# A two-layer hybrid block on one core: the retention's group norm from centred values and mean squares, its output parts added on TensorE

## What is computed

```python
def _retention(q, k, v, g, gn_w, gn_b, cos, sin):      # 4 heads of 64, 8 chunks of 128 tokens
    inner = jnp.einsum('bnihd,bnjhd->bnhij', qc, kc) * decay
    inner = jnp.einsum('bnhij,bnjhe->bnihe', inner, vc)
    # state carried over the chunks: k'v, with a decay
    cross = jnp.einsum('bnihd,nbhde->bnihe', qc, prev_states) * xi[None, None, :, :, None]
    o = (inner + cross).reshape(b, s, h, dv)
    mu = jnp.mean(o32, axis=-1, keepdims=True)
    var = jnp.mean(jnp.square(o32 - mu), axis=-1, keepdims=True)
    o = ((o32 - mu) * lax.rsqrt(var + RET_GN_EPS)).astype(dt).reshape(b, s, RET_WIDTH)
    o = o * gn_w + gn_b
    return jax.nn.silu(g) * o
```

## Time and profile before

| what | value |
|---|---|
| time, median of 3 runs | 2645.51 us (2643.24 to 2648.67) |
| the profiled execution's own time | 2646.41 us |
| its span | 2644.6 us |
| PE busy | 2555.4 us, 97% of the span |
| PEld busy | 2191.1 us, 83% |
| DVE busy | 1531.2 us, 58% |
| ACT busy | 1095.3 us, 41% |
| POOL busy | 1013.6 us, 38% |

### The profile page before, as it was taken

One profiled execution on the slowest core, in us unless ns is written; L12 is line 12 of the kernel. 1 busy time (PEld: TensorE's weight loads), 2 busy tenths in 40 slices (PEclk: granted clock), 3 DMA queues, 4 the chain that ended last, 5 costly groups with the idle time before them and its releaser, 6 DMA issues. The chain is left out here.

```text
span 2644.6 us, 43326 instructions
## 1 busy us (share of the span) xinstructions
PE 2555.4 (97%) x13188; PEld 2191.1 (83%) x13188; DVE 1531.2 (58%) x3045; ACT 1095.3 (41%) x2503; POOL 1013.6 (38%) x1161
## 2 busy tenths in 40 slices
PE   7999989999999999999999999999999999999997
PEld 6999977878788888888889998777887888888886
DVE  4667555472654455577647775555627454545785
ACT  4444554372522332344444455444634232223444
POOL 2455422174254545201044555222723545451012
PEclk8999999999999999999999999999999999999999
DMA  5111011014233233573321101012222233327533
GB/s 182 29 34 35 20 38 39 28 66 152 68 108 114 80 115 107 181 264 96 104 100 33 46 19 42 5 39 86 87 86 91 85 112 110 100 91 261 195 97 122
DMA packets 238651, 242.68 MB, mean 92 GB/s; under 512 B 27904, under 2 KB 171008, under 8 KB 238464
## 3 DMA queue, kind: packets, MB, share of 16 engines
q1 hardware_dynamic: 238464, 240.43, 28.1%
HBM read 172.75 MB, written 67.63 MB: 91 GB/s over the span
## 5 line engine op out<-in xcount | busy, mean ns | idle before, releaser
L2470 POOL TENSOR_TENSOR fw_a_lo<-fw_a_raw,fw_a_hi 128x512 fp32r<-128x512 f32 x132 | 178.8, 1355 | 457.6 <-DVE fw_s_raw L2053 457.6
L2470 POOL TENSOR_TENSOR fw_s_lo<-fw_s_raw,fw_s_hi 128x512 fp32r<-128x512 f32 x176 | 230.9, 1324 | 53.6 <-ACT fw_s_hi L1543 53.6
L733 PE MATMUL banks<-ht_hi,da_hi 128*128 128x512 f32 x496 | 193.2, 390 | 0.0
L733 PE MATMUL banks<-ht_lo,da_hi 128*128 128x512 f32 x496 | 193.2, 390 | 0.0
L733 PE MATMUL banks<-ht_hi,da_lo 128*128 128x512 f32 x496 | 193.2, 390 | 0.0
L733 PE MATMUL banks<-w_diff_hi,ht_hi 128*128 128x384 f32 x512 | 181.2, 354 | 6.1 <-DVE ht_lo L1730 4.1
L733 PE MATMUL banks<-w_diff_hi,ht_lo 128*128 128x384 f32 x512 | 173.5, 339 | 0.0
L733 PE MATMUL banks<-w_diff_lo,ht_hi 128*128 128x384 f32 x512 | 173.2, 338 | 0.0
L2298 POOL TENSOR_TENSOR qk_rot<-rope_a,rope_b 128x512 f32<-128x512 f32 x64 | 82.7, 1292 | 204.1 <-DVE rope_b L1759 204.1
L1787 DVE TENSOR_REDUCE stats<-banks 128x1 f32<-128x1024 f32 (+3 forms) x192 | 138.5, 749 | 29.3 <-PE banks L944 23.4
L1617 ACT ACTIVATE u_two<-u_two 128x512 f32<-128x512 f32 x42 | 26.6, 632 | 281.7 <-DVE u_two L2164 281.7
(11 more groups left out here) (357 smaller groups left out, 7506.8 us busy)
## 6 DMA issues: line engine op xcount, KB each, us to landing
da_raw<-act_scratch SPq DMA_DIRECT2D x154, 256.0 KB, 2.7
fw_a_raw<-in_w_gate_dram SPq DMA_DIRECT2D x88, 256.0 KB, 3.1
act_scratch<-act_s SPq DMA_DIRECT2D x66, 256.0 KB, 3.0
w_diff_raw<-in_w_in_dram SPq DMA_DIRECT2D x24, 512.0 KB, 6.4
fw_a<-in_w_up_dram SPq DMA_DIRECT2D x44, 256.0 KB, 3.2
fw_a_raw<-in_w_up_dram SPq DMA_DIRECT2D x44, 256.0 KB, 2.9
act_scratch<-act_zero SPq DMA_DIRECT2D x44, 256.0 KB, 2.4
act_scratch<-act_one SPq DMA_DIRECT2D x44, 256.0 KB, 2.8
```

What stands on the lines that cost most here:

```text
L733: mm = pe.matmul(bank, lhsT, rhs, start=first and i == 0, stop=last and i == len(pairs) - 1, skip_group_check=resumes)
L2470: pool.tensor_tensor(w[1][:], w[2][:], w[0][:].bitcast(F32), ALU.subtract).then_inc(S["f_lo"], 1)
```

## The change

The v columns are scaled while ACT copies them, with a sum of each head's 64 columns beside it, and DVE subtracts the mean of them. The output is three matmuls of 64 columns into the same 64 columns of the bank, in place of one of 128 columns and one of 64. ACT copies the sum out (`ret_take`) and squares it once for two units (`ret_squares`); DVE sums the squares, adds epsilon and scales the output (`ret_sums`, `ret_mean_squares`, `ret_normed`); `bn_stats`, `bn_aggr` and the offset are gone. POOL's root no longer adds epsilon, and `ret_finish` runs in rounds 7, 9, ..., 21. The third `keep_clock` of a round is gone; the three matmuls of `first_product` stay.

```diff
@@ TensorE @@
+        def ret_rows(j):
+            return banks[:, RET_OUT[j], 0:RET_DIM]
...
-                    fill(u, 2, RET_OUT[0])
-                    def both_parts(j, hi, lo, sides, first, last):
-                        pe.matmul(banks[:, RET_OUT[j], 0:P].rearrange("p (c d) -> p c d", c=2), hi, sides, start=first, stop=False)
-                        return pe.matmul(banks[:, RET_OUT[j], 0:64], lo, sides[:, 0, :], start=False, stop=last)
+                    if first_products_at(u):
+                        first_product(u, 2)
                     for j in range(2):
-                        mm = both_parts(j, r_at_hi[n % 2][:, tokens(j)], r_at_lo[n % 2][:, tokens(j)], rv[n % 5][:, j], True, t == 0)
+                        mm = products(ret_rows(j), split((r_at_hi[n % 2][:, tokens(j)], r_at_lo[n % 2][:, tokens(j)]),
+                                                            (rv[n % 5][:, j, 0, :], rv[n % 5][:, j, 1, :])), last=t == 0)
...
-                            mm = both_parts(j, rt_hi[n % 3][at_, 0, :], rt_lo[n % 3][at_, 0, :], state[at_, :, at_], False, True)
+                            mm = products(ret_rows(j), split((rt_hi[n % 3][at_, 0, :], rt_lo[n % 3][at_, 0, :]),
+                                                                (state[at_, 0, at_], state[at_, 1, at_])), first=False)
@@ ScalarE @@
-                def ret_normed(n):
...
-                    for j in range(2):
-                        st = act.activation(r_norm[b][:, i, 64 * j:64 * j + 64], r_sum[m % 3][:, i, j, :], ACT.Identity,
-                                            bias=r_nb[:, b, 2 * i + j:2 * i + j + 1], scale=r_rs[:, b, 2 * i + j:2 * i + j + 1])
+                def ret_take(n):
...
+                    act.activation(r_sum[m % 3][:, n % 2], banks[:, RET_OUT[0]:RET_OUT[1] + 1, 0:RET_DIM], ACT.Copy).then_inc(S["r_take"], 1)
+                def ret_squares(m):
...
+                    act.activation(r_square[:], r_sum[m % 3][:], ACT.Square).then_inc(S["r_sq"], 1)
...
-                        act.activation(r_z[n][:], banks[:, Z_BANK, :], ACT.Copy).then_inc(S["z_free"], 1)
+                        act.activation(r_z[n][:, 0:2 * P], banks[:, Z_BANK, 0:2 * P], ACT.Copy)
+                        for j in range(2):
+                            v = slice(2 * P + RET_DIM * j, 2 * P + RET_DIM * (j + 1))
+                            act.activation(r_z[n][:, v], banks[:, Z_BANK, v], ACT.Copy, scale=xz[:, n // T, j:j + 1], accum_out=v_sum[:, n, j:j + 1])
+                        act.activation(r_z[n][:, 3 * P:4 * P], banks[:, Z_BANK, 3 * P:4 * P], ACT.Copy).then_inc(S["z_free"], 1)
@@ VectorE @@
-                    dve.tensor_tensor(v, v, xz[:, n // T, 0:2].unsqueeze(2).to_broadcast([P, 2, RET_DIM]), ALU.mult)
+                    dve.scalar_tensor_tensor(v, v_sum[:, n, :].unsqueeze(2).to_broadcast([P, 2, RET_DIM]), -1.0 / RET_DIM, v, ALU.mult, ALU.add)
...
+                    dve.tensor_reduce(r_ss[:, m % 2], r_square[:], AX_X, ALU.add).then_inc(S["r_ss"], 1)
...
+                    dve.scalar_tensor_tensor(r_ms[:, b], r_ss[:, b], 1.0 / RET_DIM, xz[:, p, 2:4].unsqueeze(1).to_broadcast([P, 2, 2]),
+                                             ALU.mult, ALU.add).then_inc(S["r_ms"], 1)
...
+                    dve.tensor_tensor(r_norm[b][:].rearrange("p i (j d) -> p i j d", j=2), r_sum[m % 3][:],
+                                      r_rs[:, b].unsqueeze(3).to_broadcast([P, 2, 2, RET_DIM]), ALU.mult).then_inc(S["r_on"], 1)
@@ GpSimd @@
-                    pool.tensor_tensor(r_ms[:, b, :].rearrange("p (i j) -> p i j", i=2), mv[:, b, :, 1].rearrange("p (i j) -> p i j", i=2),
-                                       xz[:, p, 2:4].unsqueeze(1).to_broadcast([P, 2, 2]), ALU.add).then_inc(S["r_ms"], 1)
...
-                    if u >= 9 and u % 2 == 1 and u != RET_UNITS - 1:
-                        ret_finish((u - 9) // 2)
-                    if u == RET_UNITS:
-                        ret_finish((u - 10) // 2)
+                    if u >= 7 and u % 2 == 1 and (u - 7) // 2 < RET_UNITS // 2:
+                        ret_finish((u - 7) // 2)
```

More of the change, by code:

```diff
@@ L128 @@
     m_qrope=T, m_cn=T,
-    r_vlo=2 * T, r_take=2 * T, r_nb=T, r_gate=2 * T, r_kzhi=2 * T, r_kzlo=2 * T, ri_done=2 * T, r_at=2 * T, r_athi=2 * T, r_atlo=2 * T,
+    r_vlo=2 * T, r_take=2 * T, r_sq=T, r_ss=T, r_gate=2 * T, r_kzhi=2 * T, r_kzlo=2 * T, ri_done=2 * T, r_at=2 * T, r_athi=2 * T, r_atlo=2 * T,
     ro_done=2 * T, rs_done=2 * (T - 1), r_st=2 * (T - 1), r_sthi=2 * (T - 1), r_stlo=2 * (T - 1),
-    r_bn=2 * T, r_mv=2 * T, r_ms=T, r_rstd=T, r_on=2 * T, r_gw=T, r_gb=T, r_mx=T,
+    r_ms=T, r_rstd=T, r_on=T, r_gw=T, r_gb=T, r_mx=T,
     out_done=2 * T, out_add=2 * T,
@@ L304, in hybrid_block_kernel @@
     r_sum = [sb(f"r_sum{i}", [P, 2, 2, RET_DIM], F32, EREG + (12 + i) * KB) for i in range(3)]
+    r_square = sb("r_square", [P, 2, 2, RET_DIM], F32, EREG + 15 * KB)
     r_st2 = [sb(f"r_st2{i}", [P, 2, P], F32R, HT + (29 + i) * KB) for i in range(3)]
@@ L415, in hybrid_block_kernel @@
     m_rs = small(2, T)
-    bn = small(2, 2, 6)
-    mv = small(2, 4, 2)
-    r_rs = small(2, 4)
-    r_ms = small(2, 4)
-    r_nb = small(2, 4)
+    v_sum = small(2 * T, 2)
+    r_ss = small(2, 2, 2)
+    r_rs = small(2, 2, 2)
+    r_ms = small(2, 2, 2)
     minus_half = small(4)
@@ L1517, in _ @@
                 for u in RET_STEPS:
+                    if 0 <= u - 3 < RET_UNITS:
+                        ret_take(u - 3)
                     if u < RET_UNITS:
@@ L1522, in _ @@
                         ret_gate_and_v(u + 2)
-                    if 0 <= u - 7 < RET_UNITS:
-                        ret_normed(u - 7)
                     if 0 <= u - 1 < RET_UNITS:
                         ret_inner(u - 1)
+                    if u % 2 == 0 and 0 <= u // 2 - 2 < RET_UNITS // 2:
+                        ret_squares(u // 2 - 2)
                     if u in ROUND_OUT:
@@ L1965, in ret_inner, with ret_sums @@
                         st.then_inc(S["r_st"], 1)
-                def ret_take(n):
-                    m, i = n // 2, n % 2
-                    dve.wait_ge(S["ro_done"], L * PER["ro_done"] + n + 1)
-                    if m >= 3:
-                        dve.wait_ge(S["r_on"], L * PER["r_on"] + 2 * (m - 2))
-                    dve.tensor_reduce(r_sum[m % 3][:, i], banks[:, RET_OUT[0]:RET_OUT[1] + 1, 0:P].rearrange("p j (c d) -> p j d c", c=2),
-                                      AX_X, ALU.add).then_inc(S["r_take"], 1)
-                def ret_moments(n):
-                    m, i = n // 2, n % 2
-                    dve.wait_ge(S["r_take"], L * PER["r_take"] + n + 1)
-                    for j in range(2):
-                        st = dve.bn_stats(bn[:, i, j, :], r_sum[m % 3][:, i, j, :])
-                    st.then_inc(S["r_bn"], 1)
-                    dve.wait_ge(S["r_bn"], L * PER["r_bn"] + n + 1)
-                    dve.sem_inc(S["passed"], 1)
-                    for j in range(2):
-                        st = dve.bn_aggr(mv[:, m % 2, 2 * i + j, :], bn[:, i, j, :])
-                    st.then_inc(S["r_mv"], 1)
+                def ret_sums(m):
+                    dve.wait_ge(S["r_sq"], L * PER["r_sq"] + m + 1)
+                    if m >= 2:
+                        dve.wait_ge(S["r_ms"], L * PER["r_ms"] + m - 1)
+                    dve.tensor_reduce(r_ss[:, m % 2], r_square[:], AX_X, ALU.add).then_inc(S["r_ss"], 1)
                 def ret_state_low(n):
@@ L2020, in _ @@
                 for u in RET_STEPS:
-                    if 0 <= u - 3 < RET_UNITS:
-                        ret_take(u - 3)
+                    m = u // 2 - 2
+                    if u % 2 == 1 and 0 <= m < RET_UNITS // 2:
+                        ret_sums(m)
                     if u < RET_UNITS:
                         ret_low(u)
+                    if u % 2 == 1 and 0 <= m < RET_UNITS // 2:
+                        ret_mean_squares(m)
                     if 0 <= u - 1 < RET_UNITS:
                         ret_inner(u - 1)
-                    if 0 <= u - 3 < RET_UNITS:
-                        ret_moments(u - 3)
-                    if u >= 6 and u % 2 == 0 and u // 2 - 3 < RET_UNITS // 2:
-                        ret_offset(u // 2 - 3)
+                    if u % 2 == 0 and 0 <= m - 1 < RET_UNITS // 2:
+                        ret_normed(m - 1)
                     if u + 2 < RET_UNITS:
```

35 lines of the change are left out of this document (19 added, 16 removed).

## The result

| | before | after |
|---|---|---|
| median of 4 runs | 2647.06 us (2643.24 to 2648.67) | 2700.52 us (2695.94 to 2701.63) |
| ratio, 95% interval | | 1.0201 [1.0185, 1.0216] |
| profiled execution, own time | 2646.41 us | 2699.57 us |
| its mean granted clock | 0.992 | 0.974 |

The forecast was 2649.0 us with a range of 2641 to 2655. The kernel became 53.5 us slower.

A forecast was written before the change was run, and what follows sets the result against it. PE, busy for 97% of the span, was taken as the bound. Per layer, rounds -2.3 + 5.1 - 3.5 + 1.2 = +0.5 us and copy +1.2; doubled, +3.4 on 2645.5 gives 2649 us, range 2641 to 2655.

The forecast's parts named there:

- The clock falls: Rival: retention rounds at half clock for 3.4 us stretches, two a layer, +6.8 us on the sum, 2656 us; chance 0.07.
- the wait in round 11: Retention rounds: a new PE wait of 0.5 us for POOL, part of the 1.2 us a layer of new waits.
- The new wait of POOL: Round 9's state product: PE waits 0.7 us for unit 8's rk_lo, queued behind the first ret_finish moved to round 7.
- The third unread matmul: Rounds 2 to 10 and 17: removing it saves 0.23 us each, 2.3 us a layer.
- The output on PE: Retention outputs: extra matmuls paced by weight loads 0.11 us apart, 0.33 us for 14 outputs, 0.22 for two; 5.1 us a layer.
- the waits that go: Rounds 3 to 16: PE's existing waits, about half for DVE and half for POOL, disappear, saving 3.5 us a layer.
- the rival in which the extra matmuls are nearly free: Retention outputs: extra matmuls cost 25 to 30 ns each, 1.6 us a layer, giving 2643 us; chance 0.13.
- The copy in four pieces: MLA steps: ACT's copy takes 1.2 us in place of 0.60, so PE's projections wait, +1.2 us a layer.
- the waits of 0.12 us: MLA steps: three of the five projection waits a layer caused by the longer copy, 0.12 us each.
- The rival with a copy of 1.46 us: MLA steps: bank held 1.46 us, seven intervals become waits, 2.3 us a layer, 2651 us; chance 0.20.
- B: Experiments' theory, retention rounds: the clock's fall follows a single stop of PE, which comes from the order on POOL.
- A: Experiments' theory, retention rounds: the clock falls because PE has less long work with the third unread matmul gone.

The follow-up runs named there:

- kernel 7: kernel 5 with only the first ret_finish moved back to round 7: 2702.70 us, ratio 1.0210.
- kernel 8: The changed kernel with eight unread matmuls put ahead of PE's wait in round 9: 2655.00 us, ratio 1.0032.
- kernel 5: The changed kernel with the third unread matmul back and ret_finish in even rounds from 8: 2653.04 us, ratio 1.0029.
- kernel 6: The changed kernel with ret_finish in even rounds from 8, third unread matmul still out: 2652.17 us, ratio 1.0043.
- kernel 3: The kernel before with only the third unread matmul taken out of rounds 2 to 10 and 17: 2695.11 us, ratio 1.0181.
- kernel 11: The kernel before with the projected unit copied in four pieces with sums and the mean subtracted on DVE: 2646.97 us, ratio 1.0005.
- kernel 1: The changed kernel with the third unread matmul put back in rounds 2 to 10 and 17: 2697.62 us, ratio 1.0192.
- kernel 2: The changed kernel with ret_finish back in its old rounds (9, 11, 13, 16, 17, ...): 2679.16 us, ratio 1.0121.
- kernel 4: The changed kernel with the third unread matmul back and ret_finish in its old rounds: 2677.59 us, ratio 1.0106.
- kernel 12: kernel 5 with the output as before, eight matmuls and the reduction on DVE: 2649.66 us, ratio 1.0015.
- kernel 9: The kernel before with the third unread matmul kept in rounds 2 to 4, out of 5 to 10 and 17: 2647.79 us, ratio 1.0009.

## Why the prediction was wrong

**The step that failed** is the rival "The clock falls". Its mechanism was named and then dismissed at 0.07 with the reason that PE still works for over nine tenths of each round, and it was priced with two stretches of 3.4 us a layer. The share was the wrong thing to look at. In kernel 7 PE is busy for 16.00 us of the 16 from 541 us on (the first row of its table by stretch) and its clock falls behind one wait; kernel 8 has PE's useful work just as late and, by its times, mostly stays up. The size was wrong by more: the clock did not come back after one such stretch, but only 47.8 and 51.2 us later. At half clock a round took 1.80 times as long and not twice (6.34 us against 3.53 in kernel 5), so 0.80 / 1.80 = 0.44 of those 99.0 us is lost, 44 us. To this come 2 x (1.97 - 0.7) = 2.5 us of wait, and 2 x 0.5 = 1.0 us goes, the wait in round 11 that didn't appear: 45.5 us over the forecast of 2649, where 51.5 was measured. The other 6 are not accounted for; kernel 6, without a fall, lies 4 us above my terms as well (below). The reckoning is an estimate; the measurement is that kernel 6, which differs in POOL's order alone, stands 48 us lower, and that the rounds of its profiled execution are 22.9 and 23.6 us shorter in the two layers.

**The new wait of POOL, 0.7 us forecast, 1.97 measured,** was the term that set this off. Two parts of it slipped. I let POOL's start move up to 549.9; the root came at 550.58. And I took the 0.42 us that POOL waited in that stretch out of the sum, since PE would be earlier; it became 1.18 us, because the scores' high part did not come earlier, while POOL did. With these two, 550.58 + 11.2 + 1.18 = 562.96, and `rk_lo` began at 563.06. PE, too, came later to the state product than forecast, at 563.71 - 1.97 = 561.74 in place of 560.8, or the wait would have been 0.9 us longer still. The mistake is to move one engine forward and leave the chain that feeds it (PE, DVE, ACT) where it need not be asked.

**The third unread matmul, 2.3 us a layer:** the rounds of kernels 5 and 6 differ by 61.01 - (599.08 - 538.92) = 0.85 us. Kernel 6 has a wait of 0.81 us that 5 lacks, so the matmuls themselves are worth 1.7. That stretch begins at round 3 and holds nine of the ten, so it is 0.18 us each, and in round 6 alone 3.53 - 3.31 = 0.22, where 0.23 was forecast: the size was about right. What the term left out is that the removal lets PE arrive earlier at places where it then waits: in kernel 3 it turns 0.51 us into 0.74 and that costs 51 us.

**The output on PE and the waits that go.** Kernel 5 keeps the third matmul and has no waits, so my terms give it 5.1 - 3.5 = +1.6 us a layer; its rounds are 61.01 - 59.56 = 1.45 us longer. Its round 6 takes 3.53 us against 3.21, the 0.33 forecast for an output. That also settles the rival in which the extra matmuls are nearly free. In the changed kernel's round 6, on the timeline of PE, they stand as forecast:

```profile
553.18 0.28 PE L737 MATMUL banks<-rv,r_at_lo 128*128 128x64 f32 x1
553.29 0.39 PE L737 MATMUL banks<-rv,r_at_hi 128*128 128x64 f32 x2
553.51 0.28 PE L737 MATMUL banks<-rv,r_at_lo 128*128 128x64 f32 x1
```

From 553.18 to 553.51 three matmuls start, each with a weight load of its own: 0.11 us each, at 64 columns a matmul. The Trainium skill, page "TensorE: Matmul & The Clock Gate", section "Back-to-back issue gap", gives the 25 ns for a matmul by itself and says that in a stream of weight loads and matmuls both set the spacing. Here it is the spacing of the section "LDWEIGHTS" that the trace agrees with.

**The copy in four pieces, 1.2 us a layer.** The timeline of ACT in the changed kernel:

```profile
480.14 0.38 ACT L1497 ACTIVATE r_z<-banks 128x256 f32<-128x256 f32 x1 [1.95 <-PE banks L737]
480.42 0.31 ACT L1500 ACTIVATE r_z<-banks,stats 128x64 f32<-128x64 f32 x1
480.62 0.20 ACT L1500 ACTIVATION_READ_ACCUMULATOR r_z<-banks,stats 128x1 f32 x1
480.71 0.31 ACT L1500 ACTIVATE r_z<-banks,stats 128x64 f32<-128x64 f32 x1
480.91 0.21 ACT L1500 ACTIVATION_READ_ACCUMULATOR r_z<-banks,stats 128x1 f32 x1
481.00 0.28 ACT L1501 ACTIVATE r_z<-banks 128x128 f32<-128x128 f32 x1
```

From 480.14 to 481.28 is 1.14 us in place of 0.60, forecast 1.2: the bank is held for 1.62 us (479.72 to 481.34 on PE), forecast 1.68. Over the whole kernel PE waits for `r_z` four times, 2.2 us in sum, 1.1 a layer. Two projections a layer waited and not five; the waits of 0.12 us didn't show. The rival with a copy of 1.46 us fell; kernel 11 measures the whole edit at 1.0005. Yet the small costs are not all accounted for: with no fall, kernel 6 is 6.6 us above the kernel before by medians, where my terms with its wait of 0.8 give 2 x (-2.3 + 5.1 - 3.5 + 0.8 + 1.2) = +2.6. Its profiled execution, at a mean clock of 0.995 against 0.992, has a span of 2645.4 us, only 0.8 longer than before, so the short stretches at half clock outside the rounds, which vary from one execution to the next in every kernel here, are of this size too.

**Which theory stands.** B, in this form: a long stretch at half clock follows a stop of PE within these rounds (kernels 1, 2, 4 and 7 against 5 and 6). A in its strong form fell, since kernels 1 and 7 fall with the matmul in place and kernel 6 mostly doesn't without it. In a weak form, that less long work makes a shorter stop enough, it may hold, but isn't shown: kernel 3 fell behind 0.74 us in round 4, and with the matmuls in place waits of 0.77 and 0.79 us passed in kernel 12, but those were in round 11. **What stays open** is where the limit lies. A wait of 0.74 us was followed by a fall in both layers of kernel 3, ones of 0.81 and 0.79 us in kernel 6 and of 0.94 and 0.93 in kernel 4 were not, and two of 1.23 and 1.24 us went one each way in one execution of kernel 9. Just ahead of the rounds of the second layer the changed kernel itself has a longer one, on its timeline of PE, and its clock stays at 1.00 until round 9:

```profile
1867.22 0.32 PE L975 MATMUL banks<-ident,m_out 128*128 128x128 f32 x1 [1.43 <-DVE m_out L1834]
```

So the length of the stop doesn't decide alone. Nor do the runs say why kernels 8 and 12 fell behind waits of 0.30 and 0.37 us.

## What to carry to other kernels

Where PE is full with small matmuls, find every wait that an edit makes or lengthens, and price it by what the clock may do behind it: here a wait of 1.5 us cost 25 us a layer. PE's share of the span didn't show it and its busy time only grew; the row of the clock named the place. An engine at 37% can decide this by its order, so before a group of instructions is moved up, list what is queued behind it and who waits for that, with the start that the inputs of each allow. Taking work out is such an edit as well: PE then arrives sooner at a wait that stays where it is.
